# Modulation of tiles 0, 1 and the prompt as columns after the transpose, in the opening of a diffusion layer on one core

## What is computed

```python
mod = jax.nn.silu(cvec) @ w_ada + b_ada
shift1, scale1, gate1, shift2, scale2, gate2 = [m[..., None, :] for m in jnp.split(mod, 6, axis=-1)]
h = rms_norm(x, norm1_g) * (1 + scale1) + shift1
p, q, k, v = project_mixer_inputs(h, w_in, q_norm_g, k_norm_g)   # p = h @ w_in[:, :256] is the pooling part
```

## Time and profile before

| what | us |
|---|---|
| median of 3 runs (lowest, highest) | 3196.24 (3193.32, 3196.32) |
| the profiled execution | 3195.74 |
| its span in the trace | 3194.0 |
| PE busy in the span | 3092.1 (97%) |
| DVE busy | 2229.7 (70%) |
| ACT busy | 1623.1 (51%) |
| first product of the pooling projection of tile 0 starts at | 42.08 |

### The profile page before, as it was taken

The page is one execution under the profiler, slowest core; times in us unless marked ns, Lnnn a source line. Parts: engine busy times, 40 slices in busy tenths (PEclk is TensorE's granted clock), DMA queues, the critical chain, the costliest instruction groups (busy, mean ns, idle before and its releaser), DMA issues. The chain is left out here.

```text
span 3194.0 us, 67304 instructions
## 1 busy us (share of the span) xinstructions
PE 3092.1 (97%) x22490; PEld 2802.7 (88%) x22490; DVE 2229.7 (70%) x3915; ACT 1623.1 (51%) x3603; POOL 697.6 (22%) x902
## 2 busy tenths in 40 slices
PE   7989999999999999998999997999999999999999
PEld 5989989998998998997887776999999999998998
DVE  5888878888887887887884557555555555555554
ACT  4656666666666665665872225333433333333332
POOL 2532233333333333332210002111111111111111
PEclk9999999999999999999999997999999999999999
DMA  8754444345335345344335556666555555555664
GB/s 292 260 196 123 127 131 144 116 120 156 120 115 156 121 125 157 120 128 139 117 120 193 199 183 201 196 196 199 186 185 185 185 185 185 185 185 185 197 200 132
DMA packets 341256, 530.38 MB, mean 166 GB/s; under 512 B 29690, under 2 KB 256250, under 8 KB 325882
## 3 DMA queue, kind: packets, MB, share of 16 engines
q1 hardware_dynamic: 330956, 493.47, 47.0%
q0 software_dynamic: 10160, 35.13, 4.4%
HBM read 439.10 MB, written 88.64 MB: 165 GB/s over the span
## 5 line engine op out<-in xcount | busy, mean ns | idle before, releaser
L3201 PE MATMUL ps_gu<-xT,e_w 128*128 128x272 f32 x6144 | 775.9, 288 | 1.1 <-DVE xT L3399 1.1
L3201 PEld LDWEIGHTS ps_gu<-xT,e_w 128*128 128x128 f32 x6144 | 772.1, 188 | 2.5 <-issue 1.3
L1228 ACT ACTIVATE e<-ps_s,negm 128x1024 f32<-128x1024 f32 (+2 forms) x416 | 474.0, 1144 | 238.9 <-DVE negm L1658 200.8
L1643 DVE TENSOR_REDUCE mx<-ps_s 128x1 f32<-128x1024 f32 (+3 forms) x428 | 525.6, 1234 | 68.3 <-PE ps_s L849 67.4
L849 PE MATMUL ps_s<-kT,qT 128*128 128x512 f32 (+1 forms) x1920 | 479.3, 387 | 14.0 <-ACT e L1228 12.9
L3388 DVE TENSOR_TENSOR e_w<-e_raw,e_w 128x2048 fp32r<-128x2048 f32 x126 | 288.5, 2290 | 207.6 <-ACT e_w L3259 207.6
L849 PEld LDWEIGHTS ps_s<-kT,qT 128*128 128x128 f32 x1920 | 341.0, 190 | 92.5 <-ACT e L1228 33.7
L926 PE MATMUL ps_m<-w,hT 128*128 128x384 f32 x2040 | 391.0, 339 | 3.9 <-DVE o L1710 3.9
L891 PE MATMUL ps_m<-v,aT 128*128 128x128 f32 x2816 | 367.5, 277 | 1.5 <-ACT aT L1212 1.5
L926 PEld LDWEIGHTS ps_m<-w,hT 128*128 128x128 f32 x2040 | 348.3, 188 | 5.4 <-issue 5.4
L891 PEld LDWEIGHTS ps_m<-v,aT 128*128 128x128 f32 x2816 | 337.5, 191 | 5.7 <-ACT aT L1212 3.3
(11 more groups left out here) (442 smaller groups left out, 4199.1 us busy)
## 6 DMA issues: line engine op xcount, KB each, us to landing
hT<-hT_d SPq DMA_DIRECT2D x85, 1024.0 KB, 5.3
e_raw<-w_gate SPq DMA_DIRECT2D x48, 1024.0 KB, 5.2
e_raw<-w_up SPq DMA_DIRECT2D x48, 1024.0 KB, 7.5
e_raw<-w_down SPq DMA_DIRECT2D x32, 1024.0 KB, 14.8
e_raw_more<-w_down SPq DMA_DIRECT2D x32, 1024.0 KB, 7.9
tab<-tabs_d SPq DMA_DIRECT2D x85, 256.0 KB, 2.7
hT_d<-hT SPq DMA_DIRECT2D x17, 1024.0 KB, 3.9
w_lent<-w_ada SPq DMA_DIRECT2D x16, 1024.0 KB, 5.6
```

What stands on the lines that cost most here:

```text
L1228: nc.scalar.activation(out, src, ACT.Exp, bias=negm[:, s.par, c:c + 1], scale=HD ** -0.5, accum_out=acc).then_inc(exp_done.sem, 1)
L1643: nc.vector.tensor_reduce(mx[:, c, n:n + 1], ps_s[:, at:at + hi - lo], AX, ALU.max).then_inc(mx_part.sem, 1)
L3201: mm = nc.tensor.matmul(ps_gu[:, 2 * (s % 2) + f, 0:SLOTS], w_view(s, a)[:, k, f * P:f * P + P], xT[:, b, k, :], start=(k == 0 and a + b = ...
```

## The change

Six things are changed.

1. Tiles 0, 1 and 16 are modulated after the transpose. DVE only multiplies the rows by the inverse root (`scale_rows`, one TENSOR_SCALAR), PE turns them, and DVE applies scale and shift as two scalars per partition to each of the eight 128-column blocks in PSUM (`modulate_columns`), writing the result over the tile in `xt`. ACT and DVE make the high and low halves from there.
2. The columns come from `turn_columns`: four transposes for each half of `g1row` and of the shift row, and a reduction over the four groups on DVE (`sum_columns`). The spread of the prompt's rows and its copies are gone. The spread of the sample's rows stays for tiles 2 to 15.
3. PE's order in the opening changes, and with it DVE's and ACT's (below). Slab products 2 and 3 follow each other, with four transposes inside the last.
4. The split of the pooling weights is cut in two halves, interleaved with the halves of tile 0, and the pooling projection of tile 0 waits for halves.
5. SP issues the first half of slab 0 ahead of c and c_ctx; `norm1_g` goes to 8 rows instead of 128, behind x of tile 0 and behind one more memset on POOL; tables and gains move ahead of the lambdas.
6. x of tiles 4 and 5 waits for both halves of tiles 0 and 1, since the modulated tile now lies in `xt`. On ACT, `copy_pool(0)` moves ahead of the high halves of tile 1.

```diff
+            load_slab(0, slice(0, KD // 2), slab_in[0])
             with nc.allow_non_contiguous_dma(reason="1024 small constants"):
                 sp.dma_start(c_raw[:, 0, :], io["c"].rearrange("b (k p) -> p (b k)", p=P)).then_inc(c_in, 16)
                 sp.dma_start(c_raw[:, 1, :], io["c_ctx"].rearrange("(k p) -> p k", p=P)).then_inc(c_in, 16)
-            load_slab(0, slice(0, KD), slab_in[0])
+            load_slab(0, slice(KD // 2, KD), slab_in[0])
...
-            sp.dma_start(g1row, io["norm1_g"][0].partition_broadcast(P)).then_inc(g1_in, 16)
             load_x(0)
+            sp.wait_ge(blk_zero, 3)
+            for j in range(4):
+                sp.dma_start(g1row[32 * j:32 * j + 2], io["norm1_g"][0].partition_broadcast(2)).then_inc(g1_in, 16)
...
+            def scaled(t):
+                return sum(1 + KD if by_columns(x) else 2 for x in range(t)) + (1 if by_columns(t) else 2)
...
+            def turn_columns(j, half):
+                if j:
+                    pe.wait_ge(mod_done, 5 + half)
+                else:
+                    pe.wait_ge(mod_done, 2 * half + 2)
+                if half:
+                    pe.wait_ge(cols_done, 1 + j)
+                src = (g1row, mod)[j]
+                for k in range(4):
+                    lo = 512 * half + k * P
+                    mm = nc.tensor.transpose(cols_at(j, half)[:, k * P:k * P + P], src[:, lo:lo + P], g.ident[:])
+                mm.then_inc(cols_ready, 1)
 
             def turn_rows(t):
-                if t:
-                    pe.wait_ge(xs_done, 2 * t + 3)
+                pe.wait_ge(xs_done, scaled(t))
+                if t == 0:
+                    pe.wait_ge(mod_done, 4)
+                elif by_columns(t - 1):
+                    pe.wait_ge(xs_done, modulated(t - 1))
+                else:
                     pe.wait_ge(x_hi, 2 * t)
                     pe.wait_ge(x_lo, 2 * t)
...
+            def sum_columns(j, half):
+                dve.wait_ge(cols_ready, 2 * j + half + 1)
+                parts_at = cols_at(j, half).rearrange("p (k j c) -> p k c j", k=4, j=4)
+                nc.vector.tensor_reduce(cols[:, j, 4 * half:4 * half + 4, :], parts_at[:, :, 0:2, :], AX, ALU.add
+                                        ).then_inc(cols_done, 1)
+            def scale_rows(t):
+                dve.wait_ge(rinv_done, t + 1)
+                if by_columns(t):
+                    nc.vector.tensor_scalar(xt[:, t % 4, :], xt[:, t % 4, :], rinv[:, t:t + 1], None, ALU.mult
+                                            ).then_inc(xs_done, 1)
+                    return
...
+            def modulate_columns(t, halves=range(2)):
+                b = t // NS
+                dve.wait_ge(xT_ready, 2 * t + 2)
+                for half in halves:
+                    if t == 0:
+                        dve.wait_ge(cols_done, 3 + half)
+                    for k in range(4 * half, 4 * half + 4):
+                        nc.vector.tensor_scalar(xt[:, t % 4, k * P:k * P + P], ps_s[:, 1024 + k * P:1024 + k * P + P],
+                                                cols[:, 0, k, b:b + 1], cols[:, 1, k, b:b + 1], ALU.mult, ALU.add
+                                                ).then_inc(xs_done, 1)
...
                 if t == 0:
+                    modulate_columns(1)
                     low_rows(1)
                 if t + 2 < NT:
                     scale_rows(t + 2)
+                if t == NS - 1:
+                    modulate_columns(NS)
```

## The result

The changed kernel is slower: 3201.45 us (median, 3199.42 to 3204.96) against 3196.03 us of the kernel before beside it, ratio 1.0018 with a 95% interval of 1.0012 to 1.0025, so 3.8 to 8.0 us. I had forecast 1.8 us of gain and held 3197.8 to be the upper end. Its profiled span is 3200.1 us (3194.0 before).

A forecast was written before the change was run, and what follows sets the result against it. PE was taken to bound the kernel, waiting on DVE in the opening; 48.95 + 8.07 + 1.33 = 58.35 instead of 60.23 gains 1.8 us. Profiled 3195.74 less 1.8, median 0.5 higher: 3194.4 us, range 3190.2 to 3197.8.

The forecast's parts named there:

- What the opening saves on PE moves the end by as much: Behind the opening PE is busy 878.9 of 900 us, so PE time saved there was to shorten the whole equally.
- wait further back that gives the gain away: Named, without place or size, as one thing that would make the prediction wrong.
- The DMAs: Opening loads: slabs land 2.0 us sooner, from slab 0's early half, smaller `norm1_g` and a 0.4 us cost for c.
- The 1.3 us from `norm1_g`: Opening loads: `norm1_g` shrinks from 0.52 to 0.03 MB, bringing everything behind it 1.3 us forward at 386 GB/s.
- DVE's list: DVE's work from the last slab's bias to tile 2's scaled rows: 18.1 us, starting at about 30.8.
- PE's wait: Before turning tile 2, PE waits 4 to 5 us for DVE, ended by DVE's scaling.
- The half clock behind it: PE products after its new wait for DVE run at half clock, costing 1.33 us; bounds 0 and 2.3.
- The end of PE's sum: End of tile 1's projection on PE, forecast at 58.35 us; turned queries were at 60.23 before.
- Rival B: DVE's list in the opening grows through dearer blocks and scaling and a later start: 3196.9 us; chance 12%.
- Rival A: The whole 7.2 us by which tile 0's pooling starts sooner reach the end: 3189.0 us; chance 8%.
- Rival C: PE's clock stays at half through the opening, 6.0 us later, 1.8 of it eaten: 3200.4 us; chance 5%.
- What is hidden: Prompt tile's eight blocks (2.2 us) lie behind other PE work; uncovered, they would cost up to 1 us.

The follow-up runs named there:

- e5: Kernel before plus 22 idle wait instructions in DVE's program in the opening; 3200.49 us, 1.0010 against before.
- e6: Kernel before plus 37 idle wait instructions in PE's program in the opening; 3199.95 us, 1.0009 against before.
- e7: Changed kernel plus idle waits making DVE's and PE's programs each 128 instructions longer than before's; 3200.88 us, 1.0015 against before.
- e12: Changed kernel, DVE 128 and PE 64 longer, tile 1's pooling projection, queries, tile 2's low halves, tile 0's store and tile 4's load earlier; 3199.57 us, 1.0009 against before.
- e3: Changed kernel with the modulation columns kept in a tile unused until head 1, instead of their own; 3202.01 us, 1.0014 against before.
- e4: Kernel before plus an unused tile of 128 bytes per partition; 3197.78 us, 0.9998 against before.
- e8: Changed kernel with c and c_ctx issued ahead of both halves of slab 0; 3202.84 us, 1.0020 against before.
- e1: Changed kernel once more, unaltered; 3201.31 us, 1.0016 against before.
- e2: Kernel before once more, unaltered; 3198.02 us, 1.0003 against before.
- e11: Changed kernel, DVE and PE 64 longer, tile 1's pooling projected before tile 2's turn, queries normalized before scaling tile 3; 3198.72 us, 1.0006 against before.

## Why the prediction was wrong, step by step

- **"What the opening saves on PE moves the end by as much"** The earlier trace rows was the costliest step. It takes the code behind for a constant. It was not: +1.1 us in the heads' loops, +0.8 us in the output stage's (shown by e5, e6, e7, e12), and some +0.4 us between 250 and 335 us, which e3 and e5 (DVE 22 longer) have and e4 and e12 (0 and 128) don't, of the four profiles in which the clock stays full there. That is 2.3 us. My "wait further back that gives the gain away" named it only as a mishap, without place or price.
- **The DMAs** (2.0 us sooner) failed next. The third slab's product starts at 26.94 (26.84 before, 24.8 forecast). The first place in the queue was taken back by c and c_ctx, which I had put at 0.4 us: 1.7 us by the estimate above. The 1.3 us from `norm1_g` did not come either, in e8 no more than in after; e8's third product starts 0.26 us sooner than before's. What shows of the missing bytes is DMA engines that idle half the time from 27 to 28 us (0.46 busy for 1.04), not as an earlier end of a slab; what holds a slab's last part is open.
- **DVE's list** held in sum (18.07 for 18.1), starting 2.05 us late because the slabs did. Its terms did not: a block took 0.33 to 0.34 us and not 0.27, so the lone 345 ns of the earlier trace rows was the better guide and my deduction for overlap was wrong; low halves from SBUF took 1.46 for 1.29. Hand-offs cost less than the 0.5 that I had added.
- **PE's wait** was right: 5.03 us (4.6 to 5.0), ended by DVE's scaling. The half clock behind it cost 0.93 on the turn and 0.79 on the pooling, 1.72 and not 1.33, within the bounds. The end of PE's sum, 58.4 + 2.05 + 0.4, is 60.8; the projection ended at 56.32 + 4.33 = 60.65.
- **Rival B** had the right side and place and too small a size: a late start and dear blocks. **Rival A** fell to the wait. **Rival C**: the second product took 2.55 us and the third 1.92, so the clock did not stay at half. The rule on transposes (the Trainium skill, TensorE: Matmul & The Clock Gate, Part 4: PE-mode transpose) is neither borne out nor refuted here: behind the same twelve transposes and spread the third product took 1.92 us in after, where PE had then idled 1.47 us, and 2.77 in e8, where it had idled 2.20. No run has transposes alone.
- **What is hidden** held: the prompt tile, near 180 us, cost nothing that shows (by the same comparison +0.43 us from 60 to 100 us and +0.48 from 250 to 300).

The opening costs 0.4 to 1.5 us in the four profiles with after's opening and queue or c first (1.0 in the mean). With 2.3 us from the loops that is 3.3 us, short of the measured 3.8 to 8.0. One candidate for the rest is the clock. Between 250 and 300 us it has a mean of 0.97 instead of 1.00 in some profiles, worth some 1.2 us: in 7 of the 9 of kernels built on after, and 2 of the 5 on before, too few to tell by themselves. But the runs on record list their mean granted clocks: 0.9888 over the 22 runs of after and 0.9887 over the 22 of e1 and e3, against 0.9897 over the 33 of before beside e1 and e3 (but 0.9891 over the 11 of e2, the same kernel as before). Within one kernel a run with a mean clock lower by 0.001 is 1.3 us longer (the slope over all runs). By this estimate, a rough one since part of it may lie in the opening, the clock is worth some 1.2 us, and the sum of 4.5 us lies inside the measured range. That the change brings the lower clock, and by which part, is not shown: e7, e11 and e12 have 0.9901 to 0.9905, as their kernels of before (0.9900 to 0.9901). What is left stays open.

## What to carry to other kernels

A few instructions more or less ahead of a loop can lengthen the loop itself, as here by 0.8 to 1.2 us; where an edit of the opening is meant to bring a us or two, compare the loops behind it instruction by instruction before you explain the opening, and try idle waits to put them back in place. And a start bound by transfers took no gain here from another order of issue, nor from 0.5 MB less; look for the next engine in line (here DVE's list, then ACT behind a store and a load) before you count PE's head start.

## What the runs showed of the hardware

The gap behind a loop's jump back depends on how many instructions stand ahead of it: for PE 0.24 to 0.29 us at 0, 64 and 128 more, 0.35 to 0.52 at 37 more; for DVE a drift over the heads' loops of 0.2 us or less at 0 and 128 more, 0.44 at 16, 0.67 and 0.94 at 64, 1.0 to 1.2 at 22. What in the chip makes it so, no row shows. An instruction of two waits for a semaphore that is long there took 0.11 us on PE. While c's four-byte elements landed among slab 0's halves, the DMA engines of after were busy 0.87 and moved 86 GB/s; in the same stretch before moved 405 at 1.05.
